# Gate one-hots built by ScalarE instead of VectorE, and gate products per half group, in a product-key expert block

## What is computed

```
q = (xc @ w_q).reshape(128, 8, 2, 128)                # 8 heads, 2 sides
s = einsum("chsd,hskd->chsk", q, keys)                # 128 keys a side
top_s, top_i = top_k(s, 16)
best_s, best = top_k(top_s[:, :, 0, :, None] + top_s[:, :, 1, None, :], 16)
e = i1 * 128 + i2                                     # 16384 experts
g = softmax(best_s)                                   # 8 x 16 experts a token
act = gelu(einsum("cd,chkd->chk", xc, u_tab[e]))
out = einsum("chk,chkd->cd", g * act, v_tab[e])
```

## Time and profile before

| | us |
|---|---|
| runs, three | 2966.81, 2961.45, 2960.91; median 2961.45 |
| the profiled execution's own time | 2961.23 |
| its span | 2959.4 |
| PE busy | 2625.7 (89%) |
| DVE busy | 2074.1 (70%) |
| ACT busy | 700.5 (24%) |
| POOL busy | 1339.2 (45%) |
| DMA | 917.84 MB, mean 310 GB/s; granted TensorE clock 0.953 |

### The profile page before, as it was taken

The page is one execution under the profiler, slowest core; times in us unless marked ns, Lnnn a source line. Parts: engine busy times, 40 slices in busy tenths (PEclk is TensorE's granted clock), DMA queues, the critical chain, the costliest instruction groups (busy, mean ns, idle before and its releaser), DMA issues. The chain is left out here.

```text
span 2959.4 us, 36161 instructions
## 1 busy us (share of the span) xinstructions
PE 2625.7 (89%) x12550; PEld 2159.3 (73%) x12550; DVE 2074.1 (70%) x4531; ACT 700.5 (24%) x1915; POOL 1339.2 (45%) x1076
## 2 busy tenths in 40 slices
PE   4789889999999999999946879999999999999991
PEld 2544558888888878888834757888888888888880
DVE  2365249989989856666684347989979975666667
ACT  2345142134444300000005423223444410000000
POOL 0000034546567656665650005355657765555553
PEclk7889999999999999999977989999999999999995
DMA  7156133889999999999981222598999999999995
GB/s 301 65 216 272 50 116 122 336 331 384 365 377 409 409 404 409 409 409 409 409 350 64 78 97 95 216 382 325 368 351 410 409 408 405 409 409 409 409 408 200
DMA packets 246587, 917.84 MB, mean 310 GB/s; under 512 B 27120, under 2 KB 32272, under 8 KB 239120
## 3 DMA queue, kind: packets, MB, share of 16 engines
q0 software_dynamic: 147456, 536.94, 46.3%
q1 hardware_dynamic: 94800, 374.54, 32.9%
q10 hardware_dynamic: 4160, 4.19, 0.4%
HBM read 909.27 MB, written 6.29 MB: 309 GB/s over the span
## 5 line engine op out<-in xcount | busy, mean ns | idle before, releaser
L1203 PE MATMUL exp_down<-peer_gates,all_ring 128*128 128x256 f32 x2720 | 612.5, 382 | 21.4 <-DMA all_ring<-in_peer_v 21.2
L1175 PE MATMUL exp_out<-peer_both,all_ring 128*128 128x256 f32 x2752 | 615.7, 380 | 10.4 <-DMA all_ring<-in_uT 5.6
L1203 PEld LDWEIGHTS exp_down<-peer_gates,all_ring 128*128 128x128 f32 x2720 | 508.9, 190 | 114.3 <-DMA all_ring<-in_peer_v 46.7
L1175 PEld LDWEIGHTS exp_out<-peer_both,all_ring 128*128 128x128 f32 x2752 | 516.9, 190 | 87.2 <-DMA all_ring<-in_uT 12.9
L1093 POOL DMA_INDIRECT all_xT<-in_u_rows,peer_eidx x284 | 351.7, 1238 | 186.5 <-DVE peer_dots L1560 125.8
L1567 DVE SCALAR_TENSOR_TENSOR peer_both<-all_xT,peer_dots,peer_both 128x1024 f32<-128x1024 f32 x224 | 287.8, 1285 | 158.1 <-DMA all_xT<-in_peer_v,peer_eidx 154.1
L1560 DVE CUSTOM_DVE_ANT_0 all_xT<-all_xT,peer_both 128x1024 f32<-128x1024 f32 x284 | 343.6, 1219 | 29.3 <-DMA all_xT<-in_u_rows,peer_eidx 28.3
L1066 POOL TENSOR_TENSOR ask_w_lo<-all_ring,ask_w_hi 128x1024 fp32r<-128x1024 f32 x22 | 52.5, 2390 | 671.5 <-ACT ask_w_hi L1231 671.5
L1093 POOL DMA_INDIRECT all_xT<-in_peer_v,peer_eidx x228 | 259.9, 1140 | 193.8 <-DVE peer_both L1567 168.5
L1203 PE MATMUL exp_down<-peer_gates,spare_ring 128*128 128x256 f32 x1376 | 315.7, 382 | 15.2 <-DMA spare_ring<-in_peer_v 15.1
L1175 PE MATMUL exp_out<-peer_both,spare_ring 128*128 128x256 f32 x1344 | 305.4, 380 | 11.2 <-DMA spare_ring<-in_uT 7.3
...
## 6 DMA issues: line engine op xcount, KB each, us to landing
...
```

What stands on the lines that cost most here:

```text
L1175: mm = nc.tensor.matmul(outs[:, c % 2, 0:DENSE], raw[c % R][:, k, :], hd[:, k, :], start=(k == 0), stop=(k == KD - 1))
L1203: mm = nc.tensor.matmul(dn[:, m, :], raw[at % R][:, m, :], gates[:, :, c, :], start=(c == 0 and m % 2 == 0), stop=(c == NKEYS - 1), skip_g ...
```

## The change

The compares on DVE go, with `s_one`, the `hot` tiles and `HOTS_AT`. `columns(b)` now leaves -2 x index in float32 (for both sides) and the share with both signs, for each dense block in a place of its own. ACT builds the one-hots in `heavy` by itself, in float32: Abs(2n - 2 index) over the key numbers n is 0 at the key and 2 or more elsewhere; Relu(share - share x that) is the share at the key and 0 elsewhere on the first side, Relu(1 - that) is 1 or 0 on the second. TensorE multiplies one half group behind each chunk of a pair (`s_halves` counts them) instead of both behind the second, and ACT waits for the half before last instead of for the group before. All tables are placed anew. Left out below: renamed semaphores, the tile `one` passed in (a column of ones), the calls.

```diff
@@ -877,8 +877,6 @@
         self.eidx = room.sb("eidx", [P, FETCHED, HK], U32)
         self.prob = room.sb("prob", [P, FETCHED, HK])
         self.dots = room.sb("dots", [P, FETCHED, HK])
-        self.index = room.sb("index", [P, 2, P], BF16)
-        self.share = room.sb("share", [P, NB - FETCHED, P])
 
         asks = Lay(nc, f"ask{l}", at, half)
         self.w_hi = [asks.sb(f"w_hi{j}", [P, KD, P], F32R) for j in range(3)]
@@ -921,7 +919,8 @@
 
         spare = Lay(nc, f"spare{l}", split_at, 2 * KD * SEQ * 4)
         self.late = [nc.alloc_sbuf_tensor_at(f"late{l}_{j}", [P, D], F32, offset=split_at + j * D * 4) for j in range(3)]
-        self.hot = [spare.sb(f"hot{j}", [P, 2, TG // 4, NKEYS, 2], BF16) for j in range(2)]
+        self.index = spare.sb("index", [P, NB - FETCHED, 2, P])
+        self.share = spare.sb("share", [P, NB - FETCHED, 2, P])
         self.heavy = [spare.sb(f"heavy{j}", [P, 2, TG // 2, NKEYS]) for j in range(2)]
         self.back = nc.alloc_sbuf_tensor_at(f"back{l}", [P, KD, DENSE], F32, offset=spare.at)
         self.acts = [spare.sb(f"acts{j}", [P, 2, 2, P]) for j in range(4)]
...
@@ -943,9 +942,9 @@
         STEPS = 23
         ORDER = [0, 2, 1, 3]
         PAIRS = NKEYS // 2
-        NEAR = 250
+        NEAR = 262
         FIRST_DOTS = 46
-        EARLY = [(31, 0, 30), (39, 0, 44), (47, 0, 72), (55, 0, 88), (66, 64, 104), (74, 64, 120)]
+        EARLY = [(31, 0, 44), (39, 0, 60), (47, 0, 76), (55, 0, 88), (66, 60, 112), (74, 60, 128)]
 
         HEADS = [(0, 2), (2, 4), (4, PH)]
         ASK_ROUTE = {m: (0, range(8 * (m - 4), min(8 * (m - 4) + 8, STEPS))) for m in (4, 5, 6)}
@@ -955,25 +954,23 @@
         SHIFT = 1 + ASK_SLOTS[14][1]
         FIRST_ROWS = 8
 
-        GATES_AFTER = {13 + 9 * g // 5: g for g in range(GROUPS)}
-        GATES_AFTER.update({41 + 6 * g // 5: GROUPS + g for g in range(GROUPS)})
+        GATES_AFTER = {13 + 3 * g // 2: g for g in range(GROUPS)}
+        GATES_AFTER.update({38 + 3 * g // 2: GROUPS + g for g in range(GROUPS)})
         DONE_AFTER = {g: 2 * p + 2 for p, g in GATES_AFTER.items()}
         WEIGH_AFTER = {p - 1: g for p, g in GATES_AFTER.items()}
-        EXP_AFTER = {1: 0, 4: 2, 23: 1, 32: 3}
-        TURN_AFTER = {10: 2, 39: 3}
+        EXP_AFTER = {1: 0, 4: 2, 20: 1, 28: 3}
+        TURN_AFTER = {9: 2, 33: 3}
 
         ROUTE_AT = {SHIFT + n: (2, n) for n in range(STEPS)}
-        ROUTE_AT.update({SHIFT + 56 + 13 * n // 10: (1, n) for n in range(STEPS)})
-        ROUTE_AT.update({SHIFT + 88 + 15 * n // 10: (3, n) for n in range(STEPS)})
-        TOP_AT = {SHIFT + 26 + 5 * (m - 4) // 2: m for m in range(4, HS)}
-        SOFTMAX_AT = {SHIFT + 3: 0, SHIFT + 23: 2, SHIFT + 87: 1, SHIFT + 123: 3}
-        COLUMNS_AT = {SHIFT + 28: 2, SHIFT + 131: 3}
-        HOTS_AT = {SHIFT + 29 + 315 * h // 100: h for h in range(2 * GROUPS)}
-        HOTS_AT.update({SHIFT + 132 + 29 * h // 10: 2 * GROUPS + h for h in range(2 * GROUPS)})
-        SPREAD_AT = {SHIFT + 36 + 7 * g: g for g in range(GROUPS)}
-        SPREAD_AT.update({SHIFT + 144 + 59 * g // 10: GROUPS + g for g in range(GROUPS)})
+        ROUTE_AT.update({SHIFT + 50 + 13 * n // 10: (1, n) for n in range(STEPS)})
+        ROUTE_AT.update({SHIFT + 82 + 13 * n // 10: (3, n) for n in range(STEPS)})
+        TOP_AT = {SHIFT + 25 + 2 * (m - 4): m for m in range(4, HS)}
+        SOFTMAX_AT = {SHIFT + 3: 0, SHIFT + 23: 2, SHIFT + 81: 1, SHIFT + 113: 3}
+        COLUMNS_AT = {SHIFT + 28: 2, SHIFT + 121: 3}
+        SPREAD_AT = {SHIFT + 41 + 5 * g + g * g // 15: g for g in range(GROUPS)}
+        SPREAD_AT.update({SHIFT + 145 + 68 * g // 10: GROUPS + g for g in range(GROUPS)})
         POST = [p for p in range(PAIRS) if p > min(GATES_AFTER)]
-        POST_AT = {SHIFT + (41 + 37 * (p - 14) // 10 if p <= 40 else 138 + 485 * (p - 40) // 100): p for p in POST}
+        POST_AT = {SHIFT + (44 + 4 * (p - 14) if p <= 34 else 124 + 465 * (p - 34) // 100): p for p in POST}
 
         def known(p):
             n = P // TG * DB * TG
...
@@ -1089,7 +1086,7 @@
                 elif j == PICKED_ROW:
                     pool.wait_ge(s_routed, 1)
                 elif j in late_rows:
-                    pool.wait_ge(s_gmm, DB * GROUPS)
+                    pool.wait_ge(s_halves, 2 * DB * GROUPS)
                 nc.gpsimd.indirect_dma_start(
                     out=rows[j], out_offset=None, in_=t["u_rows"] if n < HALF else t["peer_v"],
                     in_offset=bass.IndirectOffsetOnAxis(ap=q.eidx[:, b, k:k + 1], axis=0)).then_inc(s_row[j], 16)
@@ -1182,17 +1179,16 @@
                     mm = nc.tensor.transpose(ps_t[:, 0, i * P:(i + 1) * P], q.pack[:, b - FETCHED, i, :], ident[:, :])
                 mm.then_inc(s_turn, 1)
 
-            def gates_of(g):
-                if g >= 2:
+            def gates_of(g, half):
+                if g >= 2 and half == 0:
                     pe.wait_ge(s_gev, g - 1)
                     pe.wait_ge(s_spread, g - 1)
-                for half in range(2):
-                    pe.wait_ge(s_hot, 2 * g + half + 1)
-                    heavy = q.heavy[half]
-                    for k in range(TG // 2):
-                        mm = nc.tensor.matmul(ps_g[g % 2][:, half * TG // 2 + k, :], heavy[:, 1, k, :],
-                                              heavy[:, 0, k, :], start=True, stop=True)
-                mm.then_inc(s_gmm, 1)
+                pe.wait_ge(s_hot, 2 * g + half + 1)
+                heavy = q.heavy[half]
+                for k in range(TG // 2):
+                    mm = nc.tensor.matmul(ps_g[g % 2][:, half * TG // 2 + k, :], heavy[:, 1, k, :],
+                                          heavy[:, 0, k, :], start=True, stop=True)
+                mm.then_inc(s_halves, 1)
 
             def down(c):
                 at = NKEYS + c
@@ -1208,8 +1204,8 @@
                 up(c)
                 if c % 2 == 1 and c // 2 in TURN_AFTER:
                     turn(TURN_AFTER[c // 2])
-                if c % 2 == 1 and c // 2 in GATES_AFTER:
-                    gates_of(GATES_AFTER[c // 2])
+                if c // 2 in GATES_AFTER:
+                    gates_of(GATES_AFTER[c // 2], c % 2)
             pe.wait_ge(s_gev, DB * GROUPS)
             pe.wait_ge(s_spread, DB * GROUPS)
             for c in range(NKEYS):
@@ -1291,23 +1287,30 @@
                             last = act.activation(gates[:, b, c, n:P], from_[:, b, n:P], ACT.Gelu_apprx_tanh)
                 last.then_inc(s_act, 1)
 
-            def weigh(g, half):
-                hot, heavy = q.hot[half], q.heavy[half]
-                if half == 0:
-                    act.wait_ge(s_share, g // GROUPS + 1)
-                act.wait_ge(s_one, 2 * g + half + 1)
-                if g >= 1:
-                    act.wait_ge(s_gmm, g)
+            def one_hots(g, half):
+                b, h, heavy = g // GROUPS, 2 * g + half, q.heavy[half]
+                first = g % GROUPS * TG + half * TG // 2
+                if h % (2 * GROUPS) == 0:
+                    act.wait_ge(s_share, b + 1)
+                if h >= 2:
+                    act.wait_ge(s_halves, h - 1)
+                for side in range(2):
+                    for k in range(TG // 2):
+                        act.activation(heavy[:, side, k, :], iota[:, :, 0], ACT.Abs, scale=2.0,
+                                       bias=q.index[:, b, side, first + k:first + k + 1]).then_inc(s_apart, 1)
                 for k in range(TG // 2):
-                    at = g % GROUPS * TG + half * TG // 2 + k
-                    act.activation(heavy[:, 0, k, :], hot[:, 0, k // 2, :, k % 2], ACT.Copy,
-                                   scale=q.share[:, g // GROUPS, at:at + 1])
-                act.activation(heavy[:, 1, :, :].rearrange("p (q k) n -> p q k n", k=2),
-                               hot[:, 1, :, :, :].rearrange("p q n k -> p q k n"),
-                               ACT.Copy).then_inc(s_hot, 1)
+                    act.wait_ge(s_apart, h * TG + k + 1)
+                    act.activation(heavy[:, 0, k, :], heavy[:, 0, k, :], ACT.Relu,
+                                   bias=q.share[:, b, 0, first + k:first + k + 1],
+                                   scale=q.share[:, b, 1, first + k:first + k + 1])
+                act.wait_ge(s_apart, (h + 1) * TG)
+                act.activation(heavy[:, 1, :, :], heavy[:, 1, :, :], ACT.Relu, bias=one[:, 0:1],
+                               scale=-1.0).then_inc(s_hot, 1)
 
             def take_gates(g):
-                act.wait_ge(s_gmm, g + 1)
+                act.wait_ge(s_halves, 2 * g + 2)
+                if g == GROUPS:
+                    act.wait_ge(s_routed, 1)
                 b, k, c = g // GROUPS, g % GROUPS, DONE_AFTER[g]
                 if c < NKEYS:
                     act.activation(gates[:, b, c:NKEYS, k * TG:(k + 1) * TG],
...
@@ -1501,27 +1504,12 @@
                     last.then_inc(s_pack, 1)
 
             def columns(b):
-                if b > FETCHED:
-                    dve.wait_ge(s_one, 2 * GROUPS)
```

(23 more changed lines are left out.)

16 lines of the change are left out of this document (7 added, 9 removed).

## The result

The changed kernel took 2933.07 us (median of four, 2929.53 to 2935.12) where the one before took 2961.18 beside it: 28.1 us less, a ratio of 0.9898 with a 95% interval of 0.9886 to 0.9910. The forecast was 2934.

The account below looks back on a forecast made before the run. DMA waste in some 250 us of each block was taken as the bound: (5 + 2.5 + 5 + 4) - 3 = 13.5 us a layer, 27 in all, so 2961.2 - 27 = 2934 us, range 2920 to 2950.

Parts of the forecast that it names:

- The bound: Late block bound by bytes at 409 GB/s; only DMA time wasted earlier can be won, 32.4 and 34.0 us in two layers.
- the thin stretches: Rest of 600 to 850 us outside the three holes: 14.6 us of DMA waste spread thin, 4 us counted back.
- the semaphore `s_routed`: GpSimd's 9.4 us wait at fetch 142; raised at slot 129 instead of 139, the 5.1 us hole comes back whole.
- the hole at spread(0): 620 to 640 us, DVE waits 8.4 us for take_gates(0): moved to slot 49, 5 of 7.0 us come back.
- The price of a half: ACT's one-hot chain per half group: eight Abs, four Relu and one wide Relu take 4.6 us, bounds 2.9 to 5.9.
- It fits with 2% to spare: Gates stretch, per three pairs: ACT needs 23.8 us against TensorE's 24.3, so ACT is no bound.
- some 4 x 0.45 us: Per three pairs, the time in which ACT waits for a half group to be multiplied.
- The charge of 3 us a layer: Deducted for DMA holes made by ACT's lost slack, late gelus and jitter at Exp and turn.
- no wait at L1531 for ACT over 2 us: Sign expected in the profile after: no single wait for ACT at that source line longer than 2 us.
- Rival A: ACT becomes the bound in the gates stretch: 3055 us, mostly 2967 to 3015, turning at 5.1 us a half; chance 0.11.
- The rule: Skill prefers VectorE, up to three times as fast, for relu; by it the move loses, with a time like 3055 us.
- Exp and turn: Exp moves to pairs 20 and 28, turn(3) to pair 33; TensorE 41 us and DVE 43 us earlier, jitter within 3 us.

Follow-up runs that it names:

- three to six more: After kernel with three, then six, more 128-wide activations on ScalarE in every half, on a tile nobody reads: ratios 1.0062 and 1.0354 to the kernel before.
- 1.5 us less a half: After kernel without the four Relus of a half that multiply the share in: median 2921.56 us, ratio 0.9869 to the kernel before.

## Why the prediction was right, point by point

**The bound** was named rightly: a block ends earlier by the DMA time no longer wasted in some 250 us of it. 26.4 us less waste by the rates of two windows, 26.1 us less time in the same two executions (28.1 by the medians), and 850 us onward untouched.

**The sum** of 27 us was right, 13.5 us a layer against 13.5 and 12.9 in the rates; **its terms were not**, and that they add up so well is luck. By the rates of layer 0, 620 to 640 us gave back 7.0 us (5 were counted), 640 to 670 us 3.9 (2.5 counted), 830 to 840 us 5.1 (5 counted): 16.0 us where 12.5 were counted. As the whole window gave 13.5, the thin stretches between lost 2.5 us, where 4 won and 3 charged make 1 us of gain. So two errors of 3.5 us cancel. The experiments show the same weakness: the semaphore `s_routed` by itself is worth about 2 us, not 5, and the hole at spread(0), cured alone in the kernel before, gave 2.5 us a layer, as the next hole grew. The step that failed is to price the holes as if each stood for itself: they share one supply of fetches, and only the rate of the whole stretch says what is won. DVE's load put back cost 4 us by the ratio, as counted, and about 6 by the rates.

**ScalarE.** The price of a half, 4.6 us, was 4.49: the overlap of neighbours held for Relus with waits on ACT's own semaphore too, two pointers cost two prices, no table load came. The balance built on it was too kind. "It fits with 2% to spare" set 23.8 us of ACT against 24.3 of TensorE; the pattern took 24.85 with ACT's chain in the lead. The mis-sized term is "some 4 x 0.45 us" of waits: ACT waits 0.5 us for a group and 2.75 for the chunk that TensorE does behind the last half product, 3.25 where 1.8 were counted. The charge of 3 us a layer was about half of what 1.5 us less a half brought back, 4 to 6. And "no wait at L1531 for ACT over 2 us" was wrong: six waits, the longest 4.3 us, because a take_gates now stands behind a one-hot group. Rival A had its mechanism right and its turning point too late, 5.1 us instead of 4.9, and past it a rise in cost is steeper than it said: from three to six more, 0.6 us a half cost 86 us, where 4 x 14.7 x 0.6 makes 35 a layer, 71 in all.

**The rule.** The Trainium skill, "ScalarE: Activation LUTs", section "Rules for kernel authors", would have left such work on VectorE. That section gives its factor of up to about three for bf16 operations with one source, a condition that the prediction left out. The trace agrees about the direction of the totals: 83.5 us less busy on DVE, 343 more on ACT. The time was decided by which engine had idle time in that stage, and ScalarE had just enough.

**Half groups** were called what makes room; without them the changed kernel is 24 us slower than the one before, so this is shown for the new tables. **Exp and turn**: little was added there (ACT's two waits at Exp are 6.1 us in layer 0, 5.0 before). **The end**: TensorE's last wait was foreseen at 20 to 28 us, and was 28.4 and 25.8.
